# Attention values held still and probabilities moved: a changed product order in the first attention of a two-block network

## The chip, the core and the metric

One Trainium2 chip, one core of it. Five engines run their own instruction streams in order and meet at semaphores: TensorE (PE, with its weight loads PEld), VectorE (DVE), ScalarE (ACT), GpSimd (POOL) and SyncE (SP, which here only issues DMA transfers). The metric is the device time of the whole program in microseconds (us).

## The reference

Two transformer-like blocks run one after the other on a sequence of 1024 positions, width 1024, in float32. Only the first block's mixer matters here: a causal convolution over half of the width, and beside it an attention with 8 heads of width 64 (three dilated windows, whose weights come together to one table of biases for each head).

```python
h = rmsnorm(x, g_mix)
z = h @ w_in                                  # zb, zc, zx, zq, zk, zv
y_c = zb * causal_dwconv3(zc * zx, conv_w, conv_b)
q, k = rmsnorm(zq), rmsnorm(zk);  v = zv      # 8 heads x 64
y_a = dilated_attention(q, k, v)              # softmax(q k^T + bias) v
y = concatenate([rmsnorm(y_c, g_out_conv), rmsnorm(y_a, g_out_attn)])
x = x + y @ w_out
```

Behind it come two large feed-forward parts, a gate, a second attention and a retention, which the change doesn't touch.

## The kernel before, in words

**Products.** A float32 product is made of three passes of a faster matrix format (`F32R`, printed as fp32r), each operand being split into a high part and a low rest: low weights by high input, high by low, high by high (lines 690 to 692). One product fills one PSUM bank (128 rows by 512 columns) from 8 slices of the input, so 24 matmuls. Plain float32 operands are also allowed; each such matmul stands in the trace as two instructions.

**The stretch that the change touches.** After the values `zv` are computed (lines 773 to 775) into all eight banks, ACT takes them to `Vt`. Then the 24 products of the convolution's inputs (4 groups `j`, three inputs `c`, `x`, `b`, two halves) run on PE, and the attention runs between them. A weave (`Weave`) holds the attention as a generator on every engine; after every second slice of a product (`pace` 2, so 4 times in a product) and once more after the product each engine takes one step of it (`tick`). After the product (`x`, 3) all that is left is run at once (`drain`).

**A step of the attention.** There are 64 units (head h, block i of 128 queries, `ATT1`), of width w = i + 1 blocks of 128 keys. In step s

- PE turns the probabilities of unit s-2 (`transpose`, line 797, into banks 6 and 7), computes the scores of unit s (lines 813 and 814, banks 4 and 5), and multiplies the probabilities of unit s-3 with the values (line 826, bank 3: probabilities `PT` stationary, values `Vt` moving, both float32, w products);
- ACT copies the turned probabilities of unit s-2 from bank 6 to `PT` (line 2466, up to 512 columns), and takes the exponential of unit s (line 2471);
- DVE takes 1/sum (line 1404), copies what stands in bank 7 (line 1408, widths over 4), adds the bias and finds the maximum for unit s (line 1416), and scales the output of unit s-3 to rows by queries (line 1426).

On ACT there also stand in this stream, per head, the cast of the next head's keys (`KSa`, line 2429, after unit i = 4), two casts of its queries (`QHa`, line 2433) and one cast of weights (`Wh`, line 2274). On DVE there stand the convolution's own steps: `ZC` (lines 1469, 1476), the taps (lines 1486 and twice 1492) and the gate (line 1507). SP loads the next head's raw keys (`KSr`, line 3542), queries and biases, and the weights `Wr` (line 3501).

**After the attention** `attention1_turn` squares the rows on ACT, computes the root, scales on ACT and DVE, turns 32 blocks on PE (line 842) and multiplies with `g_out_attn` into `KT` (line 1450). After the last convolution product, a chain on DVE, ACT and POOL makes the input of the output projection.

Of the kernel before, what the change touches and what calls it, by code (L numbers as in the profile page):

```python
# [333 lines left out]
def memory(k):  # L334
# [29 lines left out]
    k.Vt, at = put("Vt", [128, 8, 512], at)  # L364
# [3 lines left out]
    k.PT, at = put("PT", [128, 2, T], at)  # L368
# [5 lines left out]
    k.YX, at = put("YX", [128, T], at)  # L374
    k.YC, at = put("YC", [128, 2, T], at)
# [92 lines left out]
    k.YR = k.Vt.rearrange("p a b -> p (a b)").rearrange("p (k n) -> p k n", k=4)  # L468
    ga = COL["g_out_attn"]
    k.ga = k.cols[:, ga:ga + 4].rearrange("p (c n) -> p c n", n=1).to_broadcast([128, 4, 128])  # L470
# [11 lines left out]
    def ya(h):  # L482

        return k.YX[:, :] if h < 2 else k.QT[:, h // 2 - 1, :]

# [85 lines left out]
    k.hg = nc.dram_tensor("hgscr", (NF, 128, T), F32, kind="Internal").ap()  # L571
    k.hs = nc.dram_tensor("headscr", (8, 128, T), F32, kind="Internal").ap()
# [85 lines left out]
def tensor(pe, k):  # L658
# [125 lines left out]
    def attention1():  # L784
        n = len(ATT1)
        for s in range(n + 3):
            if 2 <= s <= n + 1:
# [5 lines left out]
                if i > 3 and k.wide(1, r) is not None:  # L793
                    pe.wait_ge(*at("att_ptv", 1, k.wide(1, r)))
# [21 lines left out]
            if s >= 3:  # L816
# [12 lines left out]
            yield  # L829

    def attention1_turn():
        for _ in range(19):
            yield
        for i in range(9):
            if i:
                b = (4, 6)[i % 2]
                take(b)
                pe.wait_ge(*at("yn_scaled_v", i - 1))
                pe.wait_ge(*at("yn_scaled_a", i - 1))
                for c in range(4):  # L840
                    src = k.ya(2 * c).rearrange("p (i n) -> p i n", i=8)[:, i - 1, :]
                    m = pe.transpose(ps(b)[:, 128 * c:128 * c + 128], src, ident)
                m.then_inc(*up(("full", b), "yn_turn", i - 1))
            yield
            yield

    bg.add(attention1())
    bg.add(attention1_turn())
# [398 lines left out]
def vector(dve, k):  # L1247
# [5 lines left out]
    def tick():  # L1253
        bg2.tick()
        bg.tick()
# [140 lines left out]

    def attention1():
        n = len(ATT1)
        for s in range(n + 3):
            if 2 <= s <= n + 1:  # L1400
                r = s - 2
                h, i = ATT1[r]
                dve.wait_ge(*at("att_exp", 1, r))
                dve.reciprocal(k.rx[:, r:r + 1], k.sx[:, r:r + 1]).then_inc(*up("att_rec", "att_rec", 1, r))
                if i > 3:
                    w = 128 * (i + 1) - 512
                    dve.wait_ge(*at("att_t", 1, r))
                    dve.tensor_copy(k.PT[:, r % 2, 512:512 + w], ps(7, w)).then_inc(*up("att_ptv", "att_ptv", 1, r))
# [10 lines left out]
            if s >= 3:  # L1419
                r = s - 3  # L1420
                h, i = ATT1[r]
                o = 512 * 3 + 64 * (h % 2)
                dve.wait_ge(*at("att_o", 1, r))
                dve.wait_ge(*at("att_rec", 1, r))
                out = k.ya(h).rearrange("p (i n) -> p i n", i=8)[:, i, 64 * (h % 2):64 * (h % 2) + 64]
# [4 lines left out]
    def attention1_turn():  # L1430
        for _ in range(16):
            yield
        dve.wait_ge(*at("yn_sq", 31))
        dve.tensor_reduce(k.sml[:, 80:88], k.sml[:, 0:32].rearrange("p (i n) -> p i n", i=8), mybir.AxisListType.X,
                          ALU.add).then_inc(*up("yn_v", "yn_sum"))
        dve.wait_ge(*at("yn_std"))
        dve.reciprocal(k.sml[:, 80:88], k.sml[:, 88:96]).then_inc(*up("yn_v", "yn_root"))
        yield
        for i in range(10):
            if i < 8:  # L1440
                if i == 0:
                    dve.wait_ge(*at("yn_root"))
                for c in (1, 3):
                    src = k.ya(2 * c).rearrange("p (i n) -> p i n", i=8)[:, i, :]
                    dve.tensor_scalar(src, src, k.sml[:, 80 + i:81 + i], None, ALU.mult).then_inc(
                        *up("yn_v", "yn_scaled_v" if c == 3 else "yn_one", i))
            if i > 1:
                b = (6, 4)[i % 2]
                dve.wait_ge(*at("yn_turn", i - 2))
# [2573 lines left out]
```

## Time and profile before

| what | us |
|---|---|
| median of 3 runs | 2584.46 |
| lowest and highest | 2584.06, 2586.77 |
| the profiled execution's own time | 2583.77 |
| its span in the profile | 2582.4 |
| PE busy in the span | 2534.4 (98%) |

The profile is one execution. The busy time of an engine is the time in which at least one of its instructions was under way; the start-to-start distance of neighbours tells more of what one costs. The stretch of the change runs from about 166 to 443 us of the span.

### The profile page before, as it was taken

Reading aid. Unit: us, or ns where it says so; the run is one execution under the profiler, and the core shown is the slowest. Engines: PE = TensorE matmul, PEld = TensorE weight load, DVE = VectorE, ACT = ScalarE, POOL = GpSimd, SP = SyncE. Lnnn points to the kernel's source line nnn. Section 1 sums busy time; section 2 is a strip of 40 time slices with the busy share of each in tenths; the row PEclk is TensorE's granted clock in tenths of the full one; section 3 lists DMA queues with packets and bytes.
Section 4 is the critical chain, followed back from the end, with each engine's and each line's share of the span. In section 5 each row is a group of like instructions: output and inputs, shape, how many; then the busy total and the mean of one; then the engine's idle time right before and its main releaser. Section 6 shows DMA issues by size and latency. Waiting matters only on the chain.

```text
span 2582.4 us, 35049 instructions
## 1 busy us (share of the span) xinstructions
PE 2534.4 (98%) x12474; PEld 2115.2 (82%) x12474; DVE 1309.2 (51%) x2508; ACT 1042.7 (40%) x1955; POOL 1266.7 (49%) x940
## 2 busy tenths in 40 slices
PE   8999999999999999999999999889999999999999
PEld 6888888888888888888877777689888888888887
DVE  5315446188766762225267888777247333333222
ACT  6345553253333332224256666586234333322120
POOL 2133224457666665534526454454356666656441
PEclk9999999999999999999999999999999999999999
DMA  4232312312222244220223222320422222226311
GB/s 157 75 117 91 94 54 92 145 58 106 90 82 89 74 163 171 82 66 32 101 76 93 66 62 70 108 69 21 155 74 74 82 84 80 82 105 220 116 46 70
DMA packets 90204, 238.45 MB, mean 92 GB/s; under 512 B 10256, under 2 KB 23856, under 8 KB 89776
## 3 DMA queue, kind: packets, MB, share of 16 engines
q1 hardware_dynamic: 90032, 236.21, 26.5%
q8 instruction: 101, 1.65, 0.3%
q14 instruction: 71, 0.58, 0.1%
HBM read 180.60 MB, written 51.38 MB: 90 GB/s over the span
## 4 chain that ended last, share of the span: by engine, by line
PE 90%; DVE 4%; ACT 2%; POOL 1%; issue 1%; DMA 1%; SPq 0%; ACTq 0%; DVEq 0%; POOLq 0%
PE PS L943 10%; PE PS L944 10%; PE PS L945 10%; PE PS L690 8%; PE PS L692 8%; PE PS L691 8%; PE PS L961 6%; PE PS L963 6%; PE PS L962 6%; PE PS L826 3%; PE PS L1213 2%; PE PS L1193 1%; PE PS L797 1%; PE PS L913 1%; PE PS L915 1%
## 5 line engine op out<-in xcount | busy, mean ns | idle before, releaser
L690 PE MATMUL PS<-Hh,Wl 128*128 128x512 f32 x1072 | 438.1, 409 | 12.5 <-DVE Hl L1344 10.0
L692 PE MATMUL PS<-Hh,Wh 128*128 128x512 f32 x1072 | 420.9, 393 | 0.0
L691 PE MATMUL PS<-Hl,Wh 128*128 128x512 f32 x1072 | 419.6, 391 | 0.0
L3139 POOL TENSOR_TENSOR Wl<-Wr,Wh 128x512 fp32r<-128x512 f32 (+1 forms) x158 | 210.4, 1353 | 335.7 <-ACT Wh L2274 335.6
L3243 POOL TENSOR_TENSOR RG<-RW,RG 128x512 fp32r<-128x512 f32 x176 | 247.0, 1408 | 130.1 <-ACT RG L2550 130.0
L1761 DVE TENSOR_TENSOR XA<-PS,XA 128x512 f32<-128x512 f32 x192 | 132.5, 691 | 332.2 <-PE PS L963 332.2
L961 PE MATMUL PS<-Hh,RG 128*128 128x512 f32 x704 | 274.1, 389 | 1.3 <-POOL Hl L3339 0.9
L963 PE MATMUL PS<-Hh,RG 128*128 128x512 f32 x704 | 273.9, 389 | 0.0
L962 PE MATMUL PS<-Hl,RG 128*128 128x512 f32 x704 | 273.9, 389 | 0.0
L3243 POOL TENSOR_TENSOR RG<-SW,RG 128x512 fp32r<-128x512 f32 x120 | 165.3, 1377 | 171.5 <-ACT RG L2550 146.0
L943 PE MATMUL PS<-Hh,RG 128*128 128x512 f32 x640 | 249.0, 389 | 0.0
L944 PE MATMUL PS<-Hl,RG 128*128 128x512 f32 x640 | 249.0, 389 | 0.0
L945 PE MATMUL PS<-Hh,RG 128*128 128x512 f32 x640 | 249.0, 389 | 0.0
L690 PEld LDWEIGHTS PS<-Hh,Wl 128*128 128x128 f32 x1072 | 204.7, 191 | 51.6 <-POOL Wl L3139 11.8
L692 PEld LDWEIGHTS PS<-Hh,Wh 128*128 128x128 f32 x1072 | 202.2, 189 | 44.4
L691 PEld LDWEIGHTS PS<-Hl,Wh 128*128 128x128 f32 x1072 | 203.4, 190 | 35.6 <-issue 0.2
L3332 POOL TENSOR_TENSOR RG<-R,RG 128x512 fp32r<-128x512 f32 (+1 forms) x96 | 115.7, 1212 | 204.3 <-ACT RG L2761 204.3
L943 PE MATMUL PS<-T,RG 128*128 128x512 f32 x480 | 186.8, 389 | 0.0
L945 PE MATMUL PS<-T,RG 128*128 128x512 f32 x480 | 186.7, 389 | 0.0
L944 PE MATMUL PS<-T,RG 128*128 128x512 f32 x480 | 186.7, 389 | 0.0
L2761 ACT ACTIVATE RG<-R 128x512 fp32r<-128x512 f32 (+1 forms) x96 | 56.1, 594 | 309.8 <-PE PS L963 294.1
L2550 ACT ACTIVATE RG<-RW 128x512 fp32r<-128x512 f32 x176 | 109.1, 629 | 130.0 <-PE PS L945 99.9
(358 smaller groups left out, 5139.2 us busy)
## 6 DMA issues: line engine op xcount, KB each, us to landing
RW<-in_wg SPq DMA_DIRECT2D x44, 512.0 KB, 3.6
RW<-in_wu SPq DMA_DIRECT2D x44, 512.0 KB, 4.5
R<-in_wd SPq DMA_DIRECT2D x88, 256.0 KB, 3.0
hgscr<-GB SPq DMA_DIRECT2D x44, 512.0 KB, 2.6
G<-hgscr SPq DMA_DIRECT2D x40, 512.0 KB, 6.4
Wr<-in_wi SPq DMA_DIRECT2D x27, 512.0 KB, 3.4
Wr<-in_wo SPq DMA_DIRECT2D x16, 512.0 KB, 3.4
spill<-X SPq DMA_DIRECT2D x16, 512.0 KB, 2.6
```

Source lines behind the costliest of these rows:

```text
L690: pe.matmul(ps(b), k.Wl[:, s, wc], xh[:, kx, sl], start=kk == 0, stop=False)
L691: pe.matmul(ps(b), k.Wh[:, s, wc], xl[:, kx, sl], start=False, stop=False)
L692: i = pe.matmul(ps(b), k.Wh[:, s, wc], xh[:, kx, sl], start=False, stop=kk == nk - 1)
L943: pe.matmul(ps(b), wl, xh, start=begins and kx == 0, stop=False, skip_group_check=not begins)
L944: pe.matmul(ps(b), wh, xl, start=False, stop=False, skip_group_check=not begins)
L945: i = pe.matmul(ps(b), wh, xh, start=False, stop=kx == 3, skip_group_check=not begins)
L961: pe.matmul(ps(b), wl, xh, start=q == 0, stop=False)
L962: pe.matmul(ps(b), wh, xl, start=False, stop=False)
L963: i = pe.matmul(ps(b), wh, xh, start=False, stop=q == nk - 1)
L1761: dve.tensor_tensor(XA[:, m, sl], ps(b), XA[:, m, sl], ALU.add).then_inc(*up(("free", b), "xd", tag, g, m, half))
L3139: i = pool.tensor_tensor(k.Wl[:, s, c], k.Wr[:, s, c], k.Wh[:, s, c].bitcast(F32), ALU.subtract)
L3243: pool.tensor_tensor(k.RG[:, s, 1, :], src, k.RG[:, s, 0, :].bitcast(F32), ALU.subtract).then_inc(*up("g_lo", "g_lo", tag, n))
```

## The change

- **Values.** ACT casts the values to a high part, DVE computes the low rest, into eight staged tiles `VS` that lie in space used later by other tiles. SP copies head 0's values from there to `V2[0]` and the values of heads 1 to 7 to a DRAM scratch (`valuescr`), waits until all eight are stored, and loads the later heads' values (`values_load`) one head ahead. `V2` holds for an even head (high | low), for an odd head (low | high) in 2 x 64 columns.
- **Probabilities.** ACT copies all w blocks of the turned probabilities into the high part of `PT` (from both banks); then DVE subtracts this high part from the same columns of PSUM and writes the low part beside it.
- **The product.** The values are stationary (128 x 128), the probabilities move (256 columns: high | low), in fp32r. The three useful partial sums lie in bank 3; ACT copies the one that lies on the other 64 partitions into the same bank, and DVE adds the three (`tensor_reduce`) into rows by features.
- **Norm.** 1/sum is taken once for all units at the end; it is spread to rows by 32 transposes, multiplied in by DVE, then squares, sums, root and a spread of the root by 8 transposes, and 8 multiplications into `KT`.
- **Distance.** The extra step after each product is gone; every product has 4 steps.

The core of the diff:

```diff
@@ tensor: the step's product
-                pe.wait_ge(*at("att_pt", 1, r))
-                if i > 3:
-                    pe.wait_ge(*at("att_ptv", 1, r))
+                pe.wait_ge(*at("att_lo", 1, r))
                 if h == 0:
-                    pe.wait_ge(*at("vt", i))
+                    pe.wait_ge(*at("v2_in", 0, i))
+                elif i == 0:
+                    pe.wait_ge(*at("v2_in", h))
                 for c in range(i + 1):
-                    m = pe.matmul(ps(3, 128), k.PT[:, r % 2, 128 * c:128 * c + 128],
-                                  k.Vt[:, c, 128 * (h // 2):128 * (h // 2) + 128], start=c == 0, stop=c == i)
+                    m = pe.matmul(ps(3, 256), k.V2[h % 2][:, c, :], k.PT[r % 2][:, c, :], start=c == 0, stop=c == i)
...
-                product([(u, H, ("conv", c, j, half), half == 1)], 8, half, early, pace=3 if (c, j) == ("b", 3) else 2)
-                bg.tick()
+                product([(u, H, ("conv", c, j, half), half == 1)], 8, half, early, pace=2)
@@ vector: the step
-                dve.wait_ge(*at("att_exp", 1, r))
-                dve.reciprocal(k.rx[:, r:r + 1], k.sx[:, r:r + 1]).then_inc(*up("att_rec", "att_rec", 1, r))
-                if i > 3:
-                    w = 128 * (i + 1) - 512
-                    dve.wait_ge(*at("att_t", 1, r))
-                    dve.tensor_copy(k.PT[:, r % 2, 512:512 + w], ps(7, w)).then_inc(*up("att_ptv", "att_ptv", 1, r))
+                W = 128 * (i + 1)
+                dve.wait_ge(*at("att_t", 1, r))
+                dve.wait_ge(*at("att_pt", 1, r))
+                dve.tensor_tensor(k.PT[r % 2][:, 0:i + 1, 128:256],
+                                  k.PS[:, 512 * 6:512 * 6 + W].rearrange("p (c n) -> p c n", c=i + 1),
+                                  k.PT[r % 2][:, 0:i + 1, 0:128].bitcast(F32), ALU.subtract).then_inc(
+                    *up(("free", 6), "att_lo", 1, r))
...
-                dve.tensor_scalar(out, k.PS[:, o:o + 64], k.rx[:, r:r + 1], None, ALU.mult).then_inc(
-                    *up(("free", 3), "att_y", 1, r))
+                dve.wait_ge(*at("att_c", 1, r))
+                dve.tensor_reduce(k.ya(h)[own, 128 * i:128 * i + 128],
+                                  k.PS[own, 512 * 3:512 * 3 + 384].rearrange("p (z q) -> p q z", z=3),
+                                  mybir.AxisListType.X, ALU.add).then_inc(*up(("free", 3), "att_y", 1, r))
@@ vector: the end of the norm, in the same stream as the last taps
+            for c in range(4):
+                i = dve.scalar_tensor_tensor(out=k.KT[:, c, sl], in0=k.ya(2 * c)[:, sl], scalar=col("g_out_attn", c),
+                                             in1=ps(6 + half), op0=ALU.mult, op1=ALU.mult)
@@ scalar: the step
+                act.activation(k.PT[r % 2][:, 0:i + 1, 0:128],
+                               k.PS[:, 512 * 6:512 * 6 + W].rearrange("p (c n) -> p c n", c=i + 1), ACT.Copy).then_inc(
+                    *up("att_pt", "att_pt", 1, r))
...
+                act.wait_ge(*at("att_o", 1, r))
+                act.activation(k.PS[own, 512 * 3 + 256:512 * 3 + 384], k.PS[other, 512 * 3:512 * 3 + 128],
+                               ACT.Copy).then_inc(*up("yn_a", "att_c", 1, r))
@@ sync: ahead of the convolution
+    for i in range(8):
+        v = k.VS[i][:, :, :, :].bitcast(F32).rearrange("p h z n -> p (h z n)")
+        sp.wait_ge(*at("vt", i))
+        sp.dma_start(k.V2[0][:, i, :].bitcast(F32), v[:, 0:128]).then_inc(*up(("d_s", i), "v2_in", 0, i))
+        sp.dma_start(k.vs.rearrange("h p n -> p h n")[:, 1:8, 128 * i:128 * i + 128],
+                     v[:, 128:1024].rearrange("p (h n) -> p h n", h=7)).then_inc(*up(("d_y", i), "v_kept", i))
+    for i in range(8):
+        sp.wait_ge(*at("v_kept", i))
```

DVE in a head's wide steps, before. `PP,mn<-PS` is the bias and maximum, `PT<-PS` the copy from bank 7, `QT<-PS,rx` the scaled output:

```order
L1404 RECIPROCAL rx<-sx 128x1 [waits s_att_exp]
L1408 COPY PT<-PS 128x128 [waits s_full6]
L1416 ISA PP,mn<-PS,rr 128x896 [waits s_full4]
L1416 ISA mn 128x1
L1426 TENSOR_SCALAR QT<-PS,rx 128x64 [waits s_att_rec,s_full3]
L1404 RECIPROCAL rx<-sx 128x1 [waits s_att_exp]
L1408 COPY PT<-PS 128x256 [waits s_full6]
L1416 ISA PP,mn<-PS,rr 128x1024 [waits s_full4]
```

The same steps after the change:

```order
L1443 ISA PP,mn<-PS,rr 128x896 [waits s_full4]
L1443 ISA mn 128x1
L1452 TENSOR_REDUCE QT<-PS 64x128 [waits s_yn_a,s_full3]
L1432 TENSOR_TENSOR PT_69<-PS,PT_69 128x6x128 [waits s_att_pt,s_full6]
L1443 ISA PP,mn<-PS,rr 128x1024 [waits s_full4]
L1443 ISA mn 128x1
L1452 TENSOR_REDUCE QT<-PS 64x128 [waits s_yn_a,s_full3]
```

The first item of DVE's step waits now for ACT's copy of the same unit (`s_att_pt`), and the maximum of the newest unit stands behind it.

ACT at the same place, before (`s_free4` is the maximum's signal, `s_full6` the transposes'):

```order
L2471 ACTIVATE PP,sx<-PP,mn 128x896 [waits s_free4]
L2433 ACTIVATE QHa<-QLr 128x512 [waits s_d_qb0]
L2466 ACTIVATE PT<-PS 128x512 [waits s_free6,s_full3,s_full6]
L2471 ACTIVATE PP,sx<-PP,mn 128x1024 [waits s_free4]
L2274 ACTIVATE Wh<-Wr 128x1024 [waits s_w_hi,s_w_lo,s_full2,s_d_w0]
L2466 ACTIVATE PT<-PS 128x512 [waits s_free6,s_full3,s_full6]
```

And after:

```order
L2527 ACTIVATE PP,sx<-PP,mn 128x896 [waits s_free4]
L2477 ACTIVATE QHa<-QLr 128x512 [waits s_d_qb0]
L2514 ACTIVATE PT_69<-PS 128x6x128 [waits s_full3,s_full6]
L2521 ACTIVATE PS<-PS 64x128 [waits s_full3]
L2527 ACTIVATE PP,sx<-PP,mn 128x1024 [waits s_free4]
L2318 ACTIVATE Wh<-Wr 128x1024 [waits s_w_hi,s_w_lo,s_full2,s_d_w0]
L2514 ACTIVATE PT_68<-PS 128x7x128 [waits s_full3,s_full6]
```

The copies grew to all blocks, a copy inside PSUM stands behind each, and the casts kept their places between an exponential and the next copy.

SP just ahead of the attention, after the change; the first row's eight stores go on as pairs up to `VS_84`:

```order
L3676 DMA V_64<-VS_84 128x128 [waits s_free7]
L3677 DMA valuescr<-VS_84 128x7x128
L3577 DMA Wr<-in_wc 128x1024 [waits s_d_y5,s_d_y4,s_d_y6,s_d_y3,s_d_y7,s_d_y2,s_w_lo,s_d_y1,s_d_y0]
L3618 DMA KSr<-headscr 64x1024 [waits s_q_lo]
L3618 DMA KSr<-headscr 64x1024
```

Before, the weights `Wr` and head 1's keys `KSr` stood right behind the table loads; now they stand behind the landing of all eight stores (`s_d_y0` to `s_d_y7`).

## Rows read from the trace of the kernel before

**Rows 1.** The page's busy times: engine, us, share, instructions.
```profile
PE 2534.4 (98%) x12474; PEld 2115.2 (82%) x12474; DVE 1309.2 (51%) x2508; ACT 1042.7 (40%) x1955; POOL 1266.7 (49%) x940
```
**Rows 2.** Waits, 160 to 450 us: waiter, releaser, us in total, times, longest.
```profile
DVE PT L1408 <- PE PS L797: 40.0, 25, 1.9
PE PS L813 <- DVE mn L1416: 0.5, 2, 0.2
```
**Rows 3.** Timeline of PE: start, us, instruction, count.
```profile
166.23 0.22 PE L813 MATMUL PS<-KSa,QHa 128*128 128x128 f32 x1
...
169.91 0.40 PE L690 MATMUL PS<-Hh,Wl 128*128 128x512 f32 x1
...
171.30 0.38 PE L797 MATMUL PS<-mats,PP 128*128 128x128 f32 x2
...
304.20 0.28 PE L814 MATMUL PS<-KSa,QLa 128*128 128x256 f32 x1
304.32 0.83 PE L826 MATMUL PS<-Vt,PT 128*128 128x128 f32 x6
```
**Rows 4.** The chain that ended last: start, us of the chain, what.
```profile
193.48 1.78 PE PS L826 x16
...
371.97 0.89 PE PS L826 x8
...
397.36 0.44 PE PS L842 x4
```
**Rows 5.** Groups of DVE by shape, 160 to 450 us: busy us, mean ns; idle before.
```profile
L1416 DVE CUSTOM_DVE_ANT_0 PP<-PS,rr 128x1024 f32<-128x1024 f32 x8 | 9.8, 1225 | 3.7 <-PE PS L814 3.7
L1408 DVE COPY PT<-PS 128x512 f32<-128x512 f32 x8 | 5.5, 690 | 11.5 <-PE PS L797 11.5
L1476 DVE TENSOR_TENSOR ZC<-PS,ZC 128x512 f32<-128x512 f32 x8 | 5.5, 685 | 13.7 <-PE PS L692 13.7
L1416 DVE CUSTOM_DVE_ANT_0 PP<-PS,TN 128x128 f32<-128x128 f32 x8 | 2.3, 282 | 40.1 <-PE PS L814 40.1
L1263 DVE TENSOR_TENSOR acc<-acc,K 128x512 f32<-128x512 f32 x2 | 2.1, 1031 | 1.5 <-ACT K L2298 1.5
```
**Rows 6.** Groups of ACT by shape, the same stretch.
```profile
L2466 ACT ACTIVATE PT<-PS 128x512 f32<-128x512 f32 x40 | 23.6, 590 | 25.0 <-PE PS L797 24.4
L2471 ACT ACTIVATE PP<-PP,mn 128x1024 f32<-128x1024 f32 x8 | 9.2, 1152 | 11.0 <-DVE mn L1416 11.0
L2471 ACT ACTIVATE PP<-PP,mn 128x128 f32<-128x128 f32 x8 | 3.2, 400 | 1.1 <-DVE mn L1416 1.0
L2466 ACT ACTIVATE PT<-PS 128x128 f32<-128x128 f32 x8 | 2.2, 270 | 3.4 <-PE PS L797 3.4
```
**Rows 7.** Timelines of DVE and then of ACT around one wide step.
```profile
311.82 1.22 DVE L1416 CUSTOM_DVE_ANT_0 PP<-PS,rr 128x1024 f32<-128x1024 f32 x1 [0.51 <-PE PS L814]
...
313.09 1.16 ACT L2471 ACTIVATE PP<-PP,mn 128x1024 f32<-128x1024 f32 x1 [1.60 <-DVE mn L1416]
...
319.93 0.62 ACT L2433 ACTIVATE QHa<-QLr 128x512 fp32r<-128x512 f32 x1
320.45 1.04 ACT L2274 ACTIVATE Wh<-Wr 128x1024 fp32r<-128x1024 f32 x1
321.40 0.26 ACT L2466 ACTIVATE PT<-PS 128x128 f32<-128x128 f32 x1
```
**Rows 8.** SP's timeline, then its issues: KB each, median us to landing.
```profile
158.85 0.43 SPq L3583 DMA_DIRECT2D rr<-in_T  x1
169.35 0.33 SPq L3501 DMA_DIRECT2D Wr<-in_wc  x1
...
Wr<-in_wc SPq DMA_DIRECT2D x12, 512.0 KB, 3.4
KSr<-headscr SPq DMA_DIRECT2D x16, 256.0 KB, 4.8
```
**Rows 9.** The chain that ended last, from the last taps to the output projection.
```profile
424.62 2.20 DVE YC L1492
...
443.34 0.50 PE PS L690
```

More of the change, by code:

```diff
@@ L363, in memory @@
     k.QT, at = put("QT", [128, 4, T], at)
-    k.Vt, at = put("Vt", [128, 8, 512], at)
+    k.YR, _ = put("YR", [128, 4, T], at)
+    k.V2 = [put(f"V2{z}", [128, 8, 128], at + 4 * T * z, F32R)[0] for z in range(2)]
+    early, at = at + 8 * T, at + 16 * T
     k.PP, _ = put("PP", [128, 3, T], at)
@@ L484, in ya, with sides @@
         return k.YX[:, :] if h < 2 else k.QT[:, h // 2 - 1, :]
+    def sides(h):
+        own = slice(64 * (h % 2), 64 * (h % 2) + 64)
+        return own, slice(64 - 64 * (h % 2), 128 - 64 * (h % 2))
+    k.sides = sides
+    k.CA = [k.YR[:, 2 + z // 2, half_of(z % 2)] for z in range(4)]
     def eps_at(half):
@@ L828, in attention1, with attention1_norm @@
                 m.then_inc(*up(("full", 3), "att_o", 1, r))
             yield
-    def attention1_turn():
-        for _ in range(19):
-            yield
[L834 to L843, printed above, removed]
-            yield
+    def attention1_norm():
+        yield
+        for n in range(8):
+            take(4 + n % 4)
+            pe.wait_ge(*at("y_cast", n))
+            for i in range(4):
+                m = pe.transpose(ps(4 + n % 4)[:, 128 * i:128 * i + 128], k.CA[n % 4][:, 128 * i:128 * i + 128], ident)
+            m.then_inc(*up(("full", 4 + n % 4), "y_row", n))
+            yield
+        for _ in range(6):
+            yield
+        take(4)
+        pe.wait_ge(*at("y_sum", 3))
+        for i in range(8):
+            m = pe.matmul(k.PS[:, 512 * 4 + i:512 * 4 + i + 1], k.PP[:, 2, 128 * i:128 * i + 128], col1(4, 1), start=True,
+                          stop=True)
+        m.then_inc(*up(("full", 4), "y_stat"))
+        for _ in range(4):
+            yield
+        pe.wait_ge(*at("y_root"))
+        for half in range(2):
+            take(6 + half)
+            for i in range(4):
+                r = k.sml[:, 80 + 4 * half + i:81 + 4 * half + i]
+                m = pe.transpose(ps(6 + half)[:, 128 * i:128 * i + 128], r.to_broadcast([128, 128]), ident)
+            m.then_inc(*up(("full", 6 + half), "y_spread", half))
@@ L1428, in attention1 @@
             yield
-    def attention1_turn():
-        for _ in range(16):
-            yield
[L1433 to L1437, printed above, removed]
-        yield
[L1439 to L1449, printed above, removed]
-                dve.tensor_tensor(k.KT[:, :, 128 * i - 256:128 * i - 128], ps(b).rearrange("p (c n) -> p c n", c=4), k.ga,
-                                  ALU.mult).then_inc(*up(("free", b), "yk", i - 2))
@@ new lines, in attention1_norm @@
+    def attention1_norm():
+        act.wait_ge(*at("att_rec", 1))
+        act.wait_ge(*at("att_o", 1, 63))
+        for n in range(8):
+            if n >= 4:
+                act.wait_ge(*at("y_row", n - 4))
+            c, i = n // 2, 4 * (n % 2)
+            r = k.rx[:, :].rearrange("p (h i n) -> p i h n", i=8, n=1)[:, i:i + 4, 2 * c:2 * c + 2, :]
+            act.activation(k.CA[n % 4].rearrange("p (i h n) -> p i h n", i=4, h=2), r.to_broadcast([128, 4, 2, 64]),
+                           ACT.Copy).then_inc(*up("yn_a", "y_cast", n))
@@ L2505, in scalar @@
-    bg.add(attention(1, ATT1, k.PP, k.PT, k.mn, k.sx, next_head))
-    bg.add(attention1_turn())
+            squares(c)
+        for _ in range(4):
+            yield
+        act.wait_ge(*at("y_stat"))
+        act.activation(k.sml[:, 88:96], ps(4, 8), ACT.Sqrt, bias=col("eps6")).then_inc(*up(("free", 4), "y_std"))
+        yield
+    bg.add(attention1())
+    bg.add(attention1_norm())
     def y_high(half):
         act.wait_ge(*at("conv", "b", 3, half))
-        act.wait_ge(*at("yk", 4 * half + 3))
+        act.wait_ge(*at("yk", half))
```

157 lines of the change are left out of this document (106 added, 51 removed).

## The prediction

> **What bounds the kernel now.** I read the page's busy times first, then the waits of the stretch from 160 to 450 us, then the chain and the timelines in it. PE is busy for 98% of the span [rows 1], and in the stretch it hardly ever waits: its longest wait is 0.2 us, while DVE stands idle for 40.0 us in all until PE has turned probabilities [rows 2]. So the attention is PE's, and work taken from PE there comes off the time, as long as DVE and ACT keep up. The first score matmul starts at 166.23 us [rows 3] and the last product with the values ends at 371.97 + 0.89 = 372.9 us [rows 4]: 206.7 us for 67 steps.
>
> **PE's work.** Six matmuls of a convolution product take 171.30 - 169.91 = 1.39 us [rows 3], so a product of 24 takes 5.57 us. The product with the values costs 1.78 us for 8 of them (16 instructions) [rows 4], 0.222 us each; the units hold 8 x 36 = 288. In their place stand 288 fp32r matmuls of 256 columns. The nearest row is the score matmul with 256 columns, 304.32 - 304.20 = 0.12 us before the next instruction [rows 3]; I take 0.115. That removes 288 x (0.222 - 0.115) = 30.8 us. The bounds of the new matmul are 0.11 (no cheaper than one transpose, 0.44 / 4 [rows 4]) and 0.222 (no gain). The norm has 32 transposes as before, at 0.11 each [rows 4] (3.5 us), plus 8 more and 8 one-column float32 matmuls, which I price like the transposes' pairs: 0.9 + 1.9 = 2.8 us. PE alone would gain 28.0 us. Unmeasured small parts (first matmul after a switch of format) I leave at nothing.
>
> **Where PE's steps stand afterwards.** In before, 67 steps at 5 per product spanned 13.4 products, 74.6 us; 64.0 us were the product with the values; the other 68 us, 8.5 per head, are transposes and scores. Afterwards a head (8 steps, 2 products) costs PE 8.5 + 36 x 0.115 + 11.1 = 23.7 us.
>
> **The new wait, and what is queued behind it.** DVE's low part of unit s-2 needs ACT's high part of the same unit. Behind it on DVE stands the maximum of unit s; on that waits ACT's exponential of s; and behind that on ACT stands the copy of unit s-1, for which DVE waits next. So one step has a loop through both engines: low part, maximum, exponential, any cast, copy. In before it was open: DVE's copy [rows 2] waited for PE alone. I price its parts for w blocks.
> - Maximum to exponential: 313.09 - 311.82 = 1.27 us for 8 blocks [rows 7]; for one block, by the same 0.045 beyond the instruction's own 0.282 [rows 5], 0.33. So 0.33 + 0.134 (w - 1).
> - Exponential until ACT's next start: 1.15 and 0.40 us for 8 and 1 blocks [rows 6] (the read of the sum fits in the overlap of ends). 0.40 + 0.107 (w - 1).
> - Copy: 0.27 for one, 0.59 for four blocks [rows 6], continued to eight, with 0.04 for the hand-over: 0.31 + 0.107 (w - 1).
> - Low part: no such instruction is in the trace. With one operand in PSUM and one in SBUF `ZC` takes 0.685 us for 512 columns, as the plain copy does with 0.690; with both in SBUF `acc` takes 1.031 [rows 5]. It has one in PSUM, so I take the first, 0.60 to the next start: 0.20 + 0.134 (w - 1). The second would add 0.345 / 4 = 0.086 per block.
> For one head, in which each part sees all widths 1 to 8 once, that is 8 x 1.24 + 28 x 0.482 = 23.4 us. In the loop stand also ACT's casts: `Wh` 321.40 - 320.45 = 0.95, two `QHa` at 320.45 - 319.93 = 0.52 [rows 7], and `KSa`, of `Wh`'s size, 0.95: 2.9 us. Sum 26.4. Squares of the convolution on ACT (about 0.54 twice in three heads) and taps on DVE, of 2.2 us [rows 9] twice in three heads with about half hidden behind the exponential, add 1.0. PE adds 0.8 where its own order is tighter: after an 8-block unit the transposes may start only when the low part has left banks 6 and 7, and scores wait for the maximum. So 28.2 us per head, against PE's 23.7: PE waits 4.5 us per head. The copy inside PSUM (some 0.3 us, like the one-block copy) and the sum of three parts (384 columns on 64 partitions, some 0.5 us, between 0.28 and 0.69 [rows 5]) stand outside the loop: the one falls in ACT's time behind the copy, the other in DVE's during the exponential. If that cover is gone, either costs up to 0.5 x 64 = 32 us.
>
> A page of the Trainium skill says the same of the loop's tightest part: PSUM — Partial Sum Buffer, section on bank collisions, states that two engines may not use one bank and the same partitions at once, reads included. Before, ACT read bank 6 and DVE bank 7; now both read both, so even a low part that needed no result of ACT's would have to follow the copy. No run here shows such a collision; by the rule no reordering of the two frees the loop.
>
> **The start.** SP issues the tables until 158.85 + 0.43 = 159.3 us and in before loads weights and head 1's keys at 169.35 us [rows 8]. Now all eight value stores (4.2 MB with the copies to `V2`) come between, and SP waits until the last has landed. The values come one every 1.36 us, the last ready near 166.6, so its store is issued at 167.7 at the earliest. If it lands like a 512 KB load, 3.4 us [rows 8], that is 171; if all eight pass one after the other at the pace of the key loads, 512 KB in some 5.4 us, it is 202. They are cut into 512-byte pieces, so I take neither: 3.0 us each, 24 us, hence 183.5. Weights and keys then need 0.33 + 1.1 + 4.8 us [rows 8], and head 1's keys are there at 190 (177 to 208). ACT wants them, in its stream, after the exponential of unit 4, near 177.5: it stands for 12 us (0 to 30), and with it the loop and PE. A long pause may also lower PE's clock for a while; the loop would hide that.
>
> The Trainium skill, DMA: Bandwidth & Descriptors, section Bandwidth, gives 138 GB/s for 64 KB and 341 GB/s for 1 MB transfers. By these 4.2 MB would take 12 to 30 us, an estimate by that page, and the sum would move by -9 to +9; no row here has stores in such pieces.
>
> **The end.** The last two convolution products cover PE while DVE runs the taps, which in before lead straight to the output projection at 443.34 us [rows 9]. Now five multiplications into `KT`, at 0.68 each, stand between the last `ZC` and those taps: +3.4 us (0 to 4). The rest of the norm on DVE and ACT lies beside PE's products.
>
> **The sum.** Eight heads at 28.2 are 225.6; the first two steps (no transposes yet) take 3.0 less, the last head has no casts for a next one (2.0 less), the last three steps take 6.0, the start adds 12: 238.6 us for 67 steps, which now span 16.75 products. Then 7.25 products (40.4) and the norm's PE part (6.3): 285.3. Before: 206.7 + 10.6 x 5.57 + 3.5 = 269.2. The stretch grows by 16.1, the end by 3.4: +19.5 on the profiled execution's 2583.8, 2603.3; the median stands 0.7 above it: **2604 us**.
>
> **Rivals.**
> - *PE stays the bound* (faster). The gain of PE decides if the loop is shorter than I price it, or steps overlap better. With a loop at PE's 23.7 per head, and a start of 5, it is -28.0 + 5 + 3 = -20: 2564. The point from which the change pays at all: 269.2 - 40.4 - 6.3 - 3.4 - 12 = 207.1 for 67 steps, 25.8 us per head. Against it: 26.4 are sums of measured instructions. For it: DVE is idle for long today [rows 2].
> - *The loop is at its bare sum* of 26.4 to 27 and the start costs 5: +1 to +5, near 2587. No measurable change.
> - *The subtraction runs at the pace of two SBUF operands*: 0.086 x 36 x 8 = +25: 2629.
> - *The stores are slow*: start 25 to 30 in place of 12: 2619.
> - *The change doesn't do what it says*: the new matmul, with its weight load, costs as much as the old pair. PE per head is then 27.6, still under 28.2, so the time is near the forecast's, 2604 to 2610; only the cause would differ.
>
> **How the numbers follow.** Forecast 0.56 (with its own range 2590 to 2618, and the last rival in it), slow subtraction 0.10, slow stores 0.07, bare loop 0.12, PE the bound 0.15. The range must leave out no more than 2 in 10: 2576 to 2636, which cuts the faster rival and the worst of the two slow ones together. A measurement of this kernel can tell about 0.2%, 5 us. Faster 0.15, same 0.12, slower 0.73.
>
> **What would show it.** In the profile after, the product with the values at 0.115 us each says the PE term is right. PE should wait in the attention for DVE's low part (banks 6 and 7) and DVE for ACT's copy, some 4 us per head, with heads 28 us apart. ACT should stand once for `KSr` in head 0, some 12 us. If PE's busy share stays at 98% in the stretch, or heads follow at 24 us, the loop was no bound and the forecast is wrong; if the low part takes over 1 us for four blocks, the third rival holds.

## The result and the profile after

The changed kernel takes 2622.36 us (median of 4 runs, 2621.69 to 2625.0), the kernel before 2584.26 beside it: ratio 1.0150 (95% interval 1.0137 to 1.0163), slower by 38 us. The profiled execution took 2622.1 us, 38.3 more than that of before, so the two traces can be compared as they stand. The medians of before beside the experiments lie between 2583.1 and 2584.2 us. One of the ten executions of e3 below took 7993.2 us and is left out of its ratio.

The page's busy times of the kernel after answer to [rows 1]:

```profile
PE 2533.1 (97%) x12210; PEld 2090.6 (80%) x12210; DVE 1357.3 (52%) x2479; ACT 1060.4 (40%) x1951; POOL 1263.5 (48%) x940
```

PE's busy time fell by only 1.3 us, where the forecast took 28.0 us of work from PE. Part of the difference is the lower clock at the start and the end (some 3 and 2 us, below), and part is that PE's gain was smaller than priced: in e4 and e12 below, where PE hardly waits, its busy time is 2516.3 and 2518.3 us, 18 and 16 less than before. The waits of the kernel after from 140 to 520 us (waiter, releaser: us in total, times, longest) answer to [rows 2]:

```profile
DVE PT L1432 <- ACT PT L2514: 108.0, 59, 8.8
ACT PP L2527 <- DVE mn L1443: 79.0, 63, 2.1
PEld PS L806 <- DVE PT L1432: 48.6, 42, 7.3
PE PS L806 <- DVE PT L1432: 32.0, 29, 6.9
ACT QHa L2477 <- DMA QLr<-headscr: 16.6, 7, 3.0
ACT KSa L2473 <- DMA KSr<-headscr: 6.6, 1, 6.6
```

Before, no wait of PE for DVE or ACT here was over 0.2 us. Now PE's transposes (line 806) stand 32.0 us for DVE's low part, which leaves banks 6 and 7. DVE stands for ACT's copy in 59 of 64 units, ACT for DVE's maximum in 63: the loop of the prediction. One row was not foreseen, ACT's wait for the queries `QLr`.

One round of the loop at the start of head 4 (its one-block unit; ACT, DVE, PE and then SP; start, us, instruction, in brackets the idle time before it and who ended it):

```profile
291.07 1.04 ACT L2318 ACTIVATE Wh<-Wr 128x1024 fp32r<-128x1024 f32 x1
292.02 0.90 ACT L2514 ACTIVATE PT<-PS 128x896 fp32r<-128x896 f32 x1
...
294.35 0.40 ACT L2527 ACTIVATE PP<-PP,mn 128x128 f32<-128x128 f32 x1 [1.27 <-DVE mn L1443]
...
295.30 1.03 ACT L2514 ACTIVATE PT<-PS 128x1024 fp32r<-128x1024 f32 x1 [0.45 <-PE PS L806]
296.38 0.25 ACT L2521 ACTIVATE PS<-PS 64x128 f32<-64x128 f32 x1
298.03 0.51 ACT L2527 ACTIVATE PP<-PP,mn 128x256 f32<-128x256 f32 x1 [1.41 <-DVE mn L1443]
...
300.92 0.63 ACT L2477 ACTIVATE QHa<-QLr 128x512 fp32r<-128x512 f32 x1 [2.29 <-DMA QLr<-headscr]
```

```profile
293.02 1.09 DVE L1432 TENSOR_TENSOR PT<-PS,PT 128x896 fp32r<-128x896 f32 x1 [1.82 <-ACT PT L2514]
294.03 0.28 DVE L1443 CUSTOM_DVE_ANT_0 PP<-PS,TN 128x128 f32<-128x128 f32 x1
...
294.35 0.56 DVE L1452 TENSOR_REDUCE QT<-PS 64x128 f32<-64x384 f32 x1
296.43 1.23 DVE L1432 TENSOR_TENSOR PT<-PS,PT 128x1024 fp32r<-128x1024 f32 x1 [1.52 <-ACT PT L2514]
```

```profile
294.17 1.10 PE L806 MATMUL PS<-mats,PP 128*128 128x128 f32 x8 [1.27 <-DVE PT L1432]
...
295.34 1.00 PE L835 MATMUL PS<-PT,V 128*128 128x256 f32 x7
296.18 0.40 PE L701 MATMUL PS<-Hh,Wl 128*128 128x512 f32 x1
```

```profile
294.72 0.33 SPq L3577 DMA_DIRECT2D Wr<-in_wc  x1
295.10 0.43 SPq L3642 DMA_DIRECT2D rr<-in_T  x1
295.58 1.09 SPq L3625 DMA_DIRECT2D QLr<-headscr  x2
```

Read it in order of time: the copy of 7 blocks waits behind `Wh`; the low part (293.02) follows its end by 0.10; the maximum follows at 294.03, the exponential at 294.35. PE waits for the same low part and starts its transposes at 294.17, so the copy of 8 blocks comes at 295.30. The new matmul costs (296.18 - 295.34) / 7 = 0.12 us in this row. And SP issues the load of the second half of the queries at 295.58, because the weight load `Wr` ahead of it waited for POOL, and POOL for `Wh` at 291.07. The queries are missing at 298.6, and ACT stands until 300.92 with the copy of the next unit behind it.

### The profile page after: what moved, and what is told of

Same layout as the page of the kernel before. It is cut to its first block, busy times and chain, and to the rows that moved or that the text cites. A ratio compares the mean times of both kernels' runs of the same rounds, so it can differ in the third digit from the quotient of the medians.

```text
span 2620.5 us, 34606 instructions
## 1 busy us (share of the span) xinstructions
PE 2533.1 (97%) x12210; PEld 2090.6 (80%) x12210; DVE 1357.3 (52%) x2479; ACT 1060.4 (40%) x1951; POOL 1263.5 (48%) x940
## 3 DMA queue, kind: packets, MB, share of 16 engines
q1 hardware_dynamic: 107232, 244.08, 27.5%
## 4 chain that ended last, share of the span: by engine, by line
PE 82%; DVE 5%; issue 4%; ACT 4%; DMA 3%; POOL 2%; SPq 1%; DVEq 0%; ACTq 0%; POOLq 0%
PE PS L962 10%; PE PS L964 10%; PE PS L963 10%; PE PS L701 7%; PE PS L703 7%; PE PS L702 7%; PE PS L981 6%; PE PS L982 6%; PE PS L980 6%; PE PS L1232 2%; DMA QLr<-headscr 1%; PE PS L1212 1%; POOL Wl L3216 1%; PE PS L932 1%; DVE PP L1443 1%
```

## Where the 38 us are

The one-block exponential of ACT marks each head's start: 168.90, 201.33, 231.57, 264.15, 294.35, 324.76, 356.80 and 389.03 us (the row at 294.35 above is one of them). The last product with the values (8 matmuls) starts at 421.54 and ends near 422.8; the first score matmul is at 167.11.

| part of the 67 steps | forecast | measured |
|---|---|---|
| first score matmul to first exponential | in head 0 | 1.8 |
| head 0, with the start's stall | 37.2 | 32.4 |
| heads 1 to 6 | 169.2 (28.2 each) | 187.7 (31.3 each) |
| head 7 and the last three steps | 32.2 | 33.8 |
| sum | 238.6 | 255.7 |

With 7.25 products (40.4) and the norm (6.3) behind them that is 302.4 us against 269.2 before, +33.2. What is left of the 38.3 us is 5.1, and it is not all the end. The first score matmul already stands 0.9 us later than before (167.11 against 166.23). The first addition of the output projection (line 1581 before, 1625 after) starts at 492.37 us against 452.80, 39.6 later, so the end takes 39.6 - 0.9 - 33.2 = 5.5 us. Some 1.5 us come back later, in code that the change doesn't touch. In heads 1 to 6 ACT's waits for `QLr` are 2.56, 2.26, 2.02, 2.29, 2.09 and 3.00 us, 2.4 on average. Without them a head takes 28.9 us, against the 28.2 of the forecast: the two heads in which taps and squares fall take 30.3 and 30.0, three others 27.7, 28.2 and 28.1, the sixth 29.2. The trace of e1 below, which has no such wait, agrees with 29.0 on average. Of the 0.7 that is left about 0.5 is hand-over (the low part follows the copy's start after 1.00 and 1.13 us at 7 and 8 blocks, priced 0.95 and 1.06: 8 x 0.06).

**The start.** SP, ACT and PE in the kernel after; SP's last store was issued at 173.96, and behind it stand:

```profile
178.42 0.35 SPq L3577 DMA_DIRECT2D Wr<-in_wc  x1
178.82 1.12 SPq L3618 DMA_DIRECT2D KSr<-headscr  x2
```

```profile
184.41 1.06 ACT L2473 ACTIVATE KSa<-KSr 128x1024 fp32r<-128x1024 f32 x1 [6.57 <-DMA KSr<-headscr]
```

```profile
186.93 1.33 PE L806 MATMUL PS<-mats,PP 128*128 128x128 f32 x5 [6.89 <-DVE PT L1432]
...
191.26 0.63 PE L703 MATMUL PS<-Hh,Wh 128*128 128x512 f32 x1
191.69 0.63 PE L701 MATMUL PS<-Hh,Wl 128*128 128x512 f32 x1
```

The last store had landed at 178.4 (forecast 183.5), the keys at 184.4 (190): a stall of 7, not 12. Behind it PE's matmuls of 512 columns come every 0.43 us instead of 0.23 until 192.5, the lower of the two clock levels (1.2 instead of 2.4 GHz) after 6.9 us in which PE did nothing; the granted clock from 180 to 200 us was 0.74. About 3 us go there.

**The end.** The chain of waits of the kernel after (start, us of the chain, what), which answers to [rows 9]:

```profile
462.31 3.29 DVE KT L1491 x5
465.60 1.21 DVE YC L1537
466.83 1.29 DVE YC L1537
...
468.94 0.64 ACT K L2342
469.61 0.70 DVE acc L1282
470.44 1.02 PE PS L717 x8
```

The five multiplications stand in the chain with 3.29 us, as priced. The taps (line 1537) take 1.2 to 1.3 us each here, not 2.2 (see the last section), and PE stands 2.7 us for `acc` before 470.44. Behind it eight of PE's matmuls come every 0.43 us instead of 0.23, until 476.1: 1.6 us more.

## The experiments

Each is timed against the kernel before on the same chip. "After" is the changed kernel, whose 2622.4 us the differences are taken from; e1, e2, e5, e10 and e11 are edits of it, e3, e4, e8, e9 and e12 build on one another, e6 and e7 are edits of before.

**e1: the queries ahead of the weight load.** SP loads the second half of the next head's queries a step earlier, ahead of `Wr`.

```diff
@@ sync
                 sp.dma_start(k.rr[:, :], d["T1"][h]).then_inc(*up("d_tab", "tab", h))
-                query_load(h, 1)
...
+            if i == 7 and h < 7:
+                query_load(h + 1, 1)
```

> Against the changed kernel (2622.4): only SP's order differs; the second half of a head's queries is loaded one step before the head begins, ahead of the weight load with which the equal distance now makes it coincide. In the trace of the changed kernel ACT waits 16.6 us in 7 pieces of about 2.3 us for this load, between an exponential and the next copy. Theory (the wait stands inside the loop of copy, low part, maximum and exponential, so it is paid in full): -14 to -17 us, 2606. Rival (the loop has slack there, PE or the 8-block low part comes later anyway): under 5 us off, 2618 or more.

Measured 2607.3 us, ratio 1.0094 (1.0079 to 1.0109): 15.1 less than after. The wait for `QLr` is gone, PE's for the low part falls from 32.0 to 23.4. Nearly all of the 16.6 us that ACT stood came off the time, as a delay inside a closed loop does.

**e2: the loop opened.** DVE takes the maximum of unit s before the low part of unit s-2, so that the exponential no longer waits for the low part.

```diff
@@ vector: the step
+            if s < n:
+                h, i = ATT1[s]
...
+                                         accum_out=k.mn[:, s:s + 1]).then_inc(*up(("free", 4), "att_max", 1, s))
             if 2 <= s <= n + 1:
...
                     *up(("free", 6), "att_lo", 1, r))
-            if s < n:
...
-                                         accum_out=k.mn[:, s:s + 1]).then_inc(*up(("free", 4), "att_max", 1, s))
```

> Against the changed kernel (2622.4): DVE takes the maximum of unit s ahead of the low part of unit s-2; nothing else. Theory (the loop through both engines is the bound, not the work on either): the exponential no longer stands behind copy and low part, heads fall from 31 us to about 26 or 27, so -30 to -38 us in all, 2584 to 2592. Rival (throughput: DVE and ACT simply have too much work, or the matmul's order on PE does it): order changes nothing, 2615 to 2625.

Measured 2603.3 us, ratio 1.0079 (1.0064 to 1.0094): 19.1 less than after, between the two numbers expected. The waits of e2 from 140 to 520 us say why:

```profile
DVE PT L1442 <- ACT PT L2514: 39.8, 21, 7.1
ACT QHa L2477 <- DMA QLr<-headscr: 28.9, 7, 4.6
PE PS L806 <- DVE PT L1442: 27.7, 24, 7.1
ACT PP L2527 <- DVE mn L1433: 17.3, 40, 1.3
```

The loop is open: 38 of DVE's 59 waits for the copy and 62 us of ACT's for the maximum are gone. But the faster head meets the same late load, and the wait for `QLr` grows from 16.6 to 28.9 us.

**e3: both.**

> Maximum first and queries early together. Theory: with the loop open the load's wait is mostly covered, so the two don't add: some 5 us below the maximum-first kernel, 2580 to 2587. Rival (both are independent in-line costs): the sum of the two, 2570 to 2576.

Measured 2587.9 us, ratio 1.0017 (1.0007 to 1.0027), 34.5 less than after. The two edits give 34.2 apart, so they add, which was the rival's reason and not mine; the rival's number missed because e2 alone gave less than was expected there. Removing the 28.9 us of ACT's waits in e2 gave 15.4: with the loop open, about half of such a wait is covered. Heads are 26.0 us apart.

**e4: e3, and head 1's keys ahead of the eight value stores.**

```diff
@@ sync
-            if i == 0 and h < 7:
+            if i == 0 and 0 < h < 7:
                 key_load(h + 1)
...
+    key_load(1)
     for i in range(8):
         v = k.VS[i][:, :, :, :].bitcast(F32).rearrange("p h z n -> p (h z n)")
```

> As the kernel with both, and head 1's keys are loaded ahead of the eight value stores, so that ACT doesn't stand for them (6.6 us in the changed kernel, PE 6.9 us, and half the clock for about 5 us after it). Theory: -7 to -10 us against the kernel with both. Rival (the values' own landing holds ACT or PE there as well): under 3 us.

Measured 2584.0 us, ratio 1.0003 (0.9994 to 1.0013): 3.9 less than e3, between the two numbers expected. Its trace says why it is not 7: the wait for the keys is gone, but the first half of head 1's queries is still issued behind the stores, and ACT stands 3.1 us for it before 187.92, where e3 had no such wait. Head 0 is 5.2 us shorter (25.4 instead of 30.6).

**e11: the keys early alone,** the same edit on after.

> The changed kernel with head 1's keys loaded ahead of the eight value stores, and nothing else. The forecast priced the start at 12 us; in the profile ACT waits 6.6 us for KSr, PE stands 6.9 us and then runs some 6 us at half clock. Theory (stall plus half of the slow stretch): 2611 to 2616 us. Rival (the next load behind the stores, the queries or the weights, then holds the loop up instead): 2617 to 2622 us.

Measured 2620.9 us (2619.0 to 2626.1), ratio 1.0144 (1.0131 to 1.0158): 1.5 less than after, within the spread, so the rival's number. The profiled execution is the slowest of the four (2626.1). In its trace head 1 starts at 196.9, 4.4 us earlier than in after, and the gain is lost again, most of it in head 4, where the queries are later than elsewhere:

```profile
301.37 0.63 ACT L2477 ACTIVATE QHa<-QLr 128x512 fp32r<-128x512 f32 x1 [5.38 <-DMA QLr<-headscr]
...
302.61 0.69 PE L806 MATMUL PS<-mats,PP 128*128 128x128 f32 x2 [4.01 <-DVE PT L1432]
```

That head takes 35.3 us at a granted clock of 0.90, against 30.4 at 1.00 in after. Why that load took longer isn't shown. Moving the keys is thus worth 1.5 to 4 us in total time. That is not the whole price of the start, since the queries stay behind the stores; no run moved both.

**e5: the old distance in after.** The extra step after each product is back on all five engines.

```diff
-                product([(u, H, ("conv", c, j, half), half == 1)], 8, half, early, pace=2)
+                product([(u, H, ("conv", c, j, half), half == 1)], 8, half, early, pace=3 if (c, j) == ("b", 3) else 2)
+                bg.tick()
```

> The changed kernel with one part undone: each convolution product is again followed by one extra step of the attention (5 steps per product, 3.35 products fewer beside the 67 steps, 18.7 us of PE's work that then stand behind the attention). Theory (the wait of ACT for QLr comes from the even distance, since with 8 steps per unit of weights the load Wr stands ahead of each head's rr, QLr and KSr in SP's queue; and the loop, not PE, sets the length of a head): ACT's wait for QLr falls from 16.6 to under 6 us, heads become about 2 us shorter (16 in all), the products behind the attention cost 18.7: 2615 to 2630 us. Rival (the loads are late for another reason, for instance the DMA traffic of the values): the wait for QLr stays above 12 us and the time is 2632 to 2642.

Measured 2621.8 us, ratio 1.0150 (1.0136 to 1.0164). That is the theory's number, and its reason too: the wait for `QLr` falls to 2.8 us, heads take 29.5 us instead of 31.3, and the last matmul with the values starts at 410.3 instead of 422.5, 12.2 earlier. The 18.7 us of products that now stand behind the attention are not paid in full, because they cover the norm: in after PE stands 2.7 us for the tail and has a granted clock of 0.96 from 460 to 500 us. Together nothing; some 2 us of this balance aren't assigned.

**e6: the even distance in before.** The same lines changed the other way in the kernel before.

> The kernel before with one part of the change alone: no extra step after a product, 4 steps per product, 8 per head and unit of weights. Theory (there the attention is PE's, and PE has its products as cover wherever the steps stand): within 0.2% of before, 2580 to 2590 us, although ACT's wait for QLr rises above 8 us (before 4.7), as the weight load stands ahead of it in every head. Rival (the even distance costs by itself, because the late queries hold the scores up and PE stands in order): 2592 to 2605 us, and PE waits 8 us or more for ACT or DVE in the attention.

Measured 2592.9 us, ratio 1.0036 (1.0023 to 1.0048): the rival's number, +9.8, and half of its reason. The first row is of ACT's waits in e6, the second and third are PE's, in the steps and behind them:

```profile
ACT QHa L2431 <- DMA QLr<-headscr: 32.2, 7, 5.9
```

```profile
PE PS L797 <- ACT PT L2464: 3.9, 4, 1.7
...
PE PS L842 <- DVE KT L1449: 3.6, 2, 1.9
```

So the equal distance makes the queries late here too (4.7 us before), which shows that the distance is the cause. PE covers all but 3.9 us of it. Another 3.6 us it stands behind the attention for the norm's multiplications, and with a granted clock of 0.94 from 400 to 460 us (1.00 before) it loses about 3.6 more.

**e7: the new wait alone in before.** DVE waits for ACT's copy of the same unit, without a low part.

```diff
                 dve.wait_ge(*at("att_exp", 1, r))
+                dve.wait_ge(*at("att_pt", 1, r))
```

> The kernel before with the new wait alone: at the start of its step DVE waits for ACT's copy of the turned probabilities of the same unit. The instructions stay as before, so the closed loop has only 4 blocks of copy on ACT and up to 4 on DVE: 8 x 0.33 + 28 x 0.134 = 6.4 (maximum), 6.2 (exponential), 4.4 (copy), 1.7 (copy on DVE), 2.9 casts, 1.0 squares and taps, 1.3 handovers: 23.9 us per head, against PE's 25.8. Theory (a closed loop costs only when its sum passes PE's): 2580 to 2592 us, DVE's wait for ACT's copy between 10 and 40 us. Rival (any wait between the two engines holds PE up, since the steps are unequal in width and an 8-block step is longer than PE's): 2595 to 2610 us.

Measured 2592.2 us (2587.3 to 2595.8), ratio 1.0036 (1.0024 to 1.0048). The profiled execution is its fastest, 2587.3. The waits in it:

```profile
DVE rx L1405 <- ACT PT L2467: 105.7, 61, 5.0
ACT PP L2472 <- DVE mn L1417: 74.9, 63, 2.1
PE PS L813 <- DVE mn L1417: 2.1, 7, 0.4
```

DVE waits as long for ACT's copy as in after (105.7 and 108.0 us), my range for it of 10 to 40 was far off, and yet the kernel loses 3.5 us in this execution and 9 in the median. So in this execution the same wait costs PE little where the loop is shorter than PE's work: PE waits 2.1 us for the maximum, where in after it stands 32.0 us for the low part. But the median, 2592.2, is just outside the 2580 to 2592 of the theory, and what the slower executions lose more isn't shown, since only the fastest was profiled.

**e8: e4 with the old distance.**

> The kernel with the queries early, the maximum first and head 1's keys ahead of the value stores (2584.0 us), and the old distance of 5 steps per product. Theory (the loop, still 26 to 27 us per head, is the bound in most steps, and fewer products beside the steps leave more of PE's time open): the steps get little shorter and 18.7 us of products stand behind them: 2590 to 2602 us. Rival (PE is the bound again there, and the distance is neutral): 2580 to 2588 us.

Measured 2590.9 us, ratio 1.0029 (1.0018 to 1.0041), as expected: 6.9 more than e4. Once the queries are early, the even distance is a gain, as more products stand beside the steps.

**e10 and e9: the norm's last four multiplications later.** The second half of `KT` is made behind the gate of the convolution's first half instead of ahead of the taps; e10 is that alone on after, e9 on e4.

```diff
@@ vector
-        for half in range(2):
-            sl = half_of(half)
-            dve.wait_ge(*at("y_spread", half))
-            for c in range(4):
...
+        for c in range(4):
+            norm_part(0, c)
+            yield
...
                         add("conv", 3, half, k.sq_no["conv", half, 3])
                         if half == 0:
+                            for x in range(4):
+                                norm_part(1, x)
```

> The changed kernel with that one move alone (the four multiplications of the second half into KT stand behind the gate of the convolution's first half). The forecast priced the end at 3.4 us for five of them. Theory: 2.6 us and up to 3 more by the clock: 2616 to 2620 us. Rival (the end is set by the norm's own chain, which runs late in this kernel): 2621 to 2623.

> The kernel with the queries early, the maximum first and head 1's keys ahead of the value stores (2584.0 us), and the four multiplications of the second half into KT moved on DVE from ahead of the last taps to behind the gate of the first half (after the sum of squares). Theory (they stand on the path that ends with the taps; four of them are 2.6 us, and PE then stands less long, so that the stretch at the lower clock behind it is shorter too): 2576 to 2581 us, faster than the kernel before by 0.1 to 0.3%. Rival (the low parts of the first half, which now wait behind them, or PE's idle time elsewhere take it back): 2583 to 2587 us.

e10: 2625.1 us (2616.9 to 2629.5), ratio 1.0154 (1.0137 to 1.0171), above both numbers expected; not conclusive. The 2.7 us that PE stood for `acc` are gone from its trace, but in its profiled execution, the slowest of four, two heads have waits for `QLr` of 4.5 and 4.4 us. e9: 2580.4 us, ratio 0.9986 (0.9977 to 0.9995), 3.6 less than e4: the theory's number. The four multiplications were priced at 2.6 us; the granted clock from 420 to 460 us is 1.00, where e4 had 0.91.

**e12: e9, and ACT's `Wh` one step later,** into the place where ACT waited 1.8 us.

```diff
@@ scalar
-            use()
             for half in range(2):
-                walk(8, 2, {}, tick)
+                walk(8, 2, {} if half else {2: use}, tick)
```

> The kernel with queries and keys early, the maximum first and the norm's second half late (2580.4 us), and ACT's cast Wh one step later: behind the one-block exponential, ahead of the copy of eight blocks, instead of ahead of the copy of seven. There ACT stands 1.7 to 1.8 us for PE, and PE stands 1.2 to 1.6 us for DVE's low part of seven blocks at the start of most heads. Theory (each cast in the loop costs its own length, 0.95 us; this one moves into ACT's idle time in seven heads): up to 6.6 us, 2573 to 2577 us. Rival (the loop only moves its tightest part to the copy of eight blocks, or the later weight load holds biases and keys up): 2579 to 2583 us.

Measured 2579.3 us, ratio 0.9978 (0.9969 to 0.9987). It beats both kernels, before by 0.2% and after by 43 us. Against e9 it gains 1 to 2 us, which the two intervals don't tell apart; the number is the rival's. ACT in e12 at the start of head 4:

```profile
272.04 0.39 ACT L2532 ACTIVATE PP<-PP,mn 128x128 f32<-128x128 f32 x1
...
272.43 1.05 ACT L2323 ACTIVATE Wh<-Wr 128x1024 fp32r<-128x1024 f32 x1
274.22 1.03 ACT L2519 ACTIVATE PT<-PS 128x1024 fp32r<-128x1024 f32 x1 [0.74 <-PE PS L806]
```

The cast lies in idle time now, and PE's waits of over 1 us at the heads' starts are gone (the two that remain are 0.54 and 0.67 us; 9.0 us for the low part in all). The longest that is left, 3.1 us, lies in head 0, behind ACT's wait of 3.9 us for head 1's queries. Heads are still 25.8 us apart (e4 26.0, e9 26.2), so the cast set little of them. What sets them is PE again:

```profile
274.26 0.99 PE L835 MATMUL PS<-PT,V 128*128 128x256 f32 x7
275.09 0.40 PE L701 MATMUL PS<-Hh,Wl 128*128 128x512 f32 x1
...
276.25 0.39 PE L703 MATMUL PS<-Hh,Wh 128*128 128x512 f32 x1
276.63 0.33 PE L806 MATMUL PS<-mats,PP 128*128 128x128 f32 x1
```

The table adds up such rows of PE from start to start, with the recorded waits taken out, for heads 1 to 6 (us per head). Before has 1.6 convolution products in a head, the others have 2.

| | forecast | before | after | e12 |
|---|---|---|---|---|
| product with the values | 4.1 | 7.6 | 4.7 | 4.5 |
| transposes and scores | 8.5 | 8.4 | 10.7 | 8.6 |
| convolution products | 11.1 | 9.3 | 12.1 | 12.0 |
| PE's own | 23.7 | 25.4 | 27.5 | 25.1 |
| waits | 4.5 | 0.0 | 3.8 | 0.7 |
| a head | 28.2 | 25.4 | 31.3 | 25.8 |

PE's own part in e3 and e4 is 25.0, with 1.0 of waits. In after it is larger although the work is the same; how much of that is waiting that the rows don't record as such isn't shown.

## Why the prediction was right in kind and short in size

The forecast was 2604 and the range 2576 to 2636; 2622 lies in it, on the forecast side, but +38 is twice +19.5.

- **PE's gain: right in kind, too large.** The new matmul takes 0.12 us, as priced, and the rival that it is no cheaper is out. But over heads 1 to 6 the old product took 7.6 us per head, 0.21 for each of 36, not 0.222, and the new one takes 4.5 in e12: 3.2 us per head or 25 in all, forecast 30.8. And a convolution product costs 6.0 us beside the steps, not the 5.57 read from six matmuls in a row. The step from its last matmul to the next transposes takes 0.34 us on average in e12 and 0.23 in before; what comes with such a change of kind was left at nothing. PE's own part of a head is thus 25.1 us, not 23.7. In after this is hidden, since there the loop sets the length of a head.
- **The loop: right, 0.7 us per head short.** It was the cause, shown by e2: opening it alone gives back 19 us, although it makes another wait longer. Hand-overs were under-priced (0.04 for what took 0.10), some 0.5 per head. The low part takes 1.09 us for 7 and 1.23 for 8 blocks, the pace that I chose; the rival of the slow subtraction is out. PE's waits in the rows are 3.8 us per head, 4.5 forecast. ACT's copy inside PSUM (0.25 us) and DVE's sum of three (0.56) were covered, as said.
- **The queries: the missing term.** The step that failed is "a head (8 steps, 2 products)". I used the even distance only to count products. It also makes a head exactly one unit of weights, so that `Wr`, whose load waits for POOL, always stands in SP's queue ahead of the biases, the queries and the keys that the head needs first. I counted these queues for the start and not for each head, where only ACT's cast `Wh` stands in the sum and no wait for a load. Its size is 16.6 us of waiting in after, 15.1 of time (e1). This, in heads 1 to 6, is 2.4 of the 3.1 us by which a head was too short.
- **The start: over-priced.** 12 us forecast, 7 of stall and about 3 of clock in the trace; of this the keys' part gave 1.5 (e11) to 3.9 us (e3 to e4). The stores took until 178.4 and not 183.5. The rival of the slow stores is out. The -9 to +9 us that the prediction gives for stores of 12 to 30 us would by its own sum be about -12 to +6.
- **The end: the right mechanism, 2.1 short.** The five multiplications stand in the chain with 3.29 us, priced 3.4. PE's stop of 2.7 us and the lower clock behind it were not in the sum, and the end takes 5.5. e9, which moves four of the five, gains 3.6; e10 can't tell.
- **The point from which the change pays** (25.8 us per head) holds where its other terms stay: e3, which keeps the stall at the start, has 26.0 and is 4 us behind before. e4 and e12 have less of the start, and e12 not the end, so by the same sum they should be further ahead than 0 and 5 us. The faster rival's 2564 would need 23.7 per head, which no variant reached, and PE's own 25.1 rules it out in this order of PE's work.

In sum, from the table: 19.5, plus 18.5 for six heads (14.4 of it the queries), less 3.0 for head 0 with its start, plus 1.6 for the last head and 1.7 for the rest (2.1 for the end, 0.9 ahead of the first score matmul, less 1.5 that come back later, and 0.2 by which the times differ more than the spans), is the 38.3 measured between the two profiled executions. The rival of the bare loop, 26.4 to 27 us per head, is out: even without the queries a head takes 28.9. (Its +1 to +5 us would by the prediction's own terms be -2 to +3.) That 2622 lies in the range owes something to luck: the range was drawn for other surprises (slow stores, a slow subtraction), the missing wait of the queries fell into it, and a start priced too high took 3 us off the error.

## What to carry to other kernels

Where a change takes work from the engine that bounds, price the loop of the others against the new, shorter cycle, and try the order that takes the instruction with the most followers first (here the maximum before the low part: 19 us for no extra instruction). When steps are placed at a new distance, write out what then always coincides in each in-order queue, DMA issues above all: a load that waits for its buffer holds up every load behind it, and in a fixed phase it does so each time. A wait between two engines (108 us here, 106 in e7) tells that a loop is closed, not what it costs; what it costs is read from the bounding engine's waits. And price an instruction in the company in which it will run: the start-to-start sums of a whole head gave PE's own part as 25.1 us, where single rows had given 23.7.

## What the runs showed of the hardware

**Vector instructions beside POOL.** The tap (`scalar_tensor_tensor`, two inputs in SBUF, 1024 columns) took 2.2 us as mean of the two in [rows 9], and 1.27 to 1.30 each in after. Before itself had both (2.33 and 1.28 in one pair). The same line in e6, DVE and then POOL:

```profile
217.30 2.11 DVE L1491 SCALAR_TENSOR_TENSOR YC<-ZC,cols,YC 128x1024 f32<-128x1024 f32 x1
...
225.00 1.27 DVE L1491 SCALAR_TENSOR_TENSOR YC<-ZC,cols,YC 128x1024 f32<-128x1024 f32 x1
```

```profile
215.81 2.52 POOL L3136 TENSOR_TENSOR Wl<-Wr,Wh 128x512 fp32r<-128x512 f32 x2 [3.18 <-ACT Wh L2272]
...
227.67 1.28 POOL L3191 TENSOR_TENSOR QLa<-QLr,QHa 128x512 fp32r<-128x512 f32 x1 [9.33 <-ACT QHa L2431]
```

The slow tap starts while POOL's second subtraction runs, the quick one while POOL is idle. In before, POOL's pair of subtractions at 424.12 took 3.83 us instead of 2.54, beside two taps. In after the steps stand so that POOL is idle beside the taps. The Trainium skill, SBUF — State Buffer, section Who interferes with whom, says that a DVE instruction with two SBUF inputs contends with a GpSimd instruction that reads SBUF; the trace agrees, at 0.8 to 1.05 us for one tap. I had priced the taps at the slow value.

**The clock after a short stop.** 6.9 us without work brought PE to its lower level for about 6 us of work, and in heads with a stop of 3 to 4 us (e10, e11) the granted clock of the head was 0.90 to 0.95. In after itself it was 0.94 and 0.95 in heads 3 and 6, where the longest single stops were 2.1 and 1.6 us. A stall of PE thus can cost more than its length, at the start by some 40%. The runs of e10 spread over 12.6 us, and the fastest has a mean granted clock of 0.997, the slowest of 0.993.
